# The differential branch's next V moved among the scores, and softmax scaling of three more branches moved onto the probabilities

## What is computed

```
def dense_attend(q, k, v):                       # MLA branch, 8 heads
    s = einsum('bqhd,bkhd->bhqk', q * (q.shape[-1] ** -0.5), k)
    p = softmax(s)
    return einsum('bhqk,bkhd->bqhd', p, v)

def diff_attend(q, k, v, lam):                   # differential branch, 8 heads
    s = einsum('bqhmd,bkhmd->bhmqk', q * (DIFF_HD ** -0.5), k)
    p = softmax(s)
    a = p[:, :, 0] - lam * p[:, :, 1]
    return einsum('bhqk,bkhd->bqhd', a, v)
# then rms_norm(o, subln) * (1 - lam_init)

# swa branch: 16 query heads on 4 key heads, window 128, a sink in the softmax
yz = y * silu(z);  terms += sigmoid(g) * (yz @ w_branch[r])
```

## Time and profile before

| | |
|---|---|
| time, median of 3 runs | 4425.87 us (4422.62 to 4426.99) |
| the profiled execution | 4427.5 us |
| its span in the profile | 4425.7 us |
| TensorE busy | 3882.1 us, 88% (21165 matmuls) |
| weight loads busy | 2965.3 us, 67% |
| VectorE busy | 2101.5 us, 47% (3225 instructions) |
| ScalarE busy | 1384.6 us, 31% (2472 instructions) |
| GpSimd busy | 0.2 us |
| mean granted TensorE clock | 0.946 |
| moved by DMA | 275.36 MB |

### The profile page before, as it was taken

How to read it: one execution, slowest core, us unless ns; L and a number is a source line. 1 busy time by engine, 2 the same in 40 slices (tenths; PEclk the granted TensorE clock), 3 DMA queues, 4 the chain that set the end, 5 groups by cost and what they waited for, 6 DMA issues and landing times. The chain is left out here.

```text
span 4425.7 us, 56278 instructions
## 1 busy us (share of the span) xinstructions
PE 3882.1 (88%) x21165; PEld 2965.3 (67%) x21165; DVE 2101.5 (47%) x3225; ACT 1384.6 (31%) x2472; POOL 0.2 (0%) x4
## 2 busy tenths in 40 slices
PE   5988979996699999999798998977999999798888
PEld 2665758874466787777586766765667666585666
DVE  2444345543444425667524554333453666535544
ACT  2433233322133313444312433221332444313432
POOL 0000000000000000000000000000000000000000
PEclk8999989998799999999899999988999999899999
DMA  6443325531101021111121101211103111131122
GB/s 231 132 120 86 95 85 167 166 104 53 29 24 28 24 62 39 33 38 38 29 62 34 29 25 34 62 40 35 32 27 86 42 44 43 38 76 34 34 56 73
DMA packets 504242, 275.36 MB, mean 62 GB/s; under 512 B 56666, under 2 KB 489782, under 8 KB 504095
## 3 DMA queue, kind: packets, MB, share of 16 engines
q1 hardware_dynamic: 483186, 252.08, 20.3%
q10 hardware_dynamic: 20908, 21.26, 1.5%
HBM read 271.08 MB, written 10.32 MB: 64 GB/s over the span
## 5 line engine op out<-in xcount | busy, mean ns | idle before, releaser
L559 PE MATMUL ps<-h_high,w_high 128*128 128x512 f32 (+1 forms) x3512 | 1334.6, 380 | 187.3 <-DVEq L2249 130.7
L559 PE MATMUL ps<-h_low,w_high 128*128 128x512 f32 (+1 forms) x3512 | 1282.5, 365 | 0.0
L559 PE MATMUL ps<-h_high,w_low 128*128 128x512 f32 (+1 forms) x3512 | 1279.0, 364 | 0.0
L559 PEld LDWEIGHTS ps<-h_high,w_high 128*128 128x128 f32 x3512 | 673.8, 192 | 349.4 <-DVEq L2249 137.9
L555 DVE TENSOR_TENSOR w_low<-w_raw,w_high 128x1024 fp32r<-128x1024 f32 x378 | 453.6, 1200 | 626.8 <-ACT w_high L545 606.9
L559 PEld LDWEIGHTS ps<-h_low,w_high 128*128 128x128 f32 x3512 | 674.9, 192 | 105.6 <-issue 11.7
L559 PEld LDWEIGHTS ps<-h_high,w_low 128*128 128x128 f32 x3512 | 673.2, 192 | 106.6
L545 ACT ACTIVATE w_high<-w_raw 128x1024 fp32r<-128x1024 f32 x378 | 392.4, 1039 | 796.3 <-PE ps L559 610.0
L778 ACT ACTIVATE probs<-ps,neg_max 128x768 f32<-128x768 f32 (+2 forms) x368 | 288.8, 788 | 469.5 <-DVE neg_max L803 268.7
L559 PE MATMUL ps<-k_high,q_high 64*128 64x256 f32 (+4 forms) x784 | 189.9, 403 | 152.5 <-ACT probs L778 100.9
L559 PE MATMUL ps<-probsT,v 128*128 128x512 f32 (+4 forms) x736 | 286.9, 559 | 5.2 <-DVE probsT L986 4.8
(11 more groups left out here) (197 smaller groups left out, 3948.4 us busy)
## 6 DMA issues: line engine op xcount, KB each, us to landing
w_raw<-in_w_in SPq DMA_DIRECT2D x444, 256.0 KB, 3.1
y_and_merged<-in_w_mod SPq DMA_DIRECT2D x96, 256.0 KB, 3.1
w_raw<-in_w_branch SPq DMA_DIRECT2D x96, 256.0 KB, 3.1
w_raw<-in_w_up SPq DMA_DIRECT2D x88, 256.0 KB, 4.2
y_and_merged<-in_w_ada SPq DMA_DIRECT2D x64, 256.0 KB, 3.4
w_raw<-in_w_out SPq DMA_DIRECT2D x48, 256.0 KB, 3.1
w_raw<-in_w_down SPq DMA_DIRECT2D x44, 256.0 KB, 2.9
y_and_merged<-in_w_ada SPq DMA_DIRECT2D x4, 2048.0 KB, 20.4
```

Of the source, the lines that this page charges most:

```text
L559: return nc.tensor.matmul(*a, **kw)
```

## The change

Two parts. First, `SCALED_LAST` holds `swa` alone. `dil`, `na` and `mla` so go the way of `diff`: each item's probabilities are scaled by VectorE before they are transposed, one item behind the maxima (in pairs in the twin branches), the waits before the values are for `normed`, and the spreading matmuls, the common reciprocal and the multiplication of Z are gone for them. Second, in `diff` the 16 steps of the next V stand behind Q and K in the side work of the scores: 48 steps instead of 32 in layer 0, 40 instead of 24 in layer 1. To free PSUM banks 0 and 1 for them, ScalarE copies Q out amid the exponentials, behind the item at which `side_plan` has the Q steps done (`act_q_out`, semaphore `q_out`); the rotation of Q goes to bank 3; V's features go to a slot of YM instead of EB. ScalarE copies V after the first chunk's copy; the transposes of V stand right behind the value products, then the sums of squares, then Z's projection. On VectorE the copy of V's transposes comes ahead of the output. The epilogues have no side work, before and after.

```diff
-SCALED_LAST = ("dil", "na", "mla", "swa")
+SCALED_LAST = ("swa",)
...
                 maxima(idx)
-            inverses()
+                if idx and s["name"] not in SCALED_LAST:
+                    normalise(idx - 1)
+            if s["name"] in SCALED_LAST:
+                inverses()
+            else:
+                normalise(n - 1)
...
-            pe.wait_ge(S["exped"], cnt(s, "exped", t, per * s["items"], (u + 1) * s["items"]))
+            if s["name"] in SCALED_LAST:
+                pe.wait_ge(S["exped"], cnt(s, "exped", t, per * s["items"], (u + 1) * s["items"]))
+            else:
+                pe.wait_ge(S["normed"], cnt(s, "normed", t, per * s["items"], (u + 1) * s["items"]))
...
-            spread_inverses(pe, s, t, u)
+            if s["name"] in SCALED_LAST:
+                spread_inverses(pe, s, t, u)
             product(n - 1)
-            if s["cq"]:
+            if s["name"] in SCALED_LAST and s["cq"]:
                 spread_context(pe, s)
...
-            at = min([g for g in range(s["items"] // size) if done_by(s, q + k, g) >= q] + [s["items"]])
-            return q + k, size * (at + 1)
+            v = 16 if s["name"] == "diff" else 0
+            at = min([g for g in range(s["items"] // size) if done_by(s, q + k + v, g) >= q] + [s["items"]])
+            return q + k + v, size * (at + 1)
...
+            b = 3 if name == "diff" else 0
+            mm(PS[0:rows, 512 * b:512 * b + 512], rot[:, :], Q[0:rows, 0:LAT], start=True, stop=True).then_inc(S["rope_mm"], 1)
...
+                pe.wait_ge(S["q_out"], cnt(s, "q_out", t, ui, u + 1))
                 yield from split_steps(pe, s, t, 4, 2, 128, tgroups(0, True))
...
-            return PP[:, 4096:4608] if s["first"] else EB[:, 1, :]
+            return PP[:, 4096:4608] if s["first"] else YM[:, 13 * TOK:14 * TOK]
...
+        def act_q_out(act, s, t, u):
+
+            act.wait_ge(s_h, cnt(s, "h", t, 4, 1))
+            for d, p in evac_cols(s, 0, Q, s["cq"]):
+                last = act.activation(d, p, ACT.Copy, scale=SCALE["diff"])
+            last.then_inc(S["q_out"], 1)
...
             if s["first"]:
                 yk = i + (0 if name == "dil" else 4)
-                v.tensor_tensor(Y[:, yk, 0:LAT], bank(5), Z[:, 0:LAT], ALU.mult).then_inc(S["y"], 1)
+                v.tensor_copy(Y[:, yk, 0:LAT], bank(5)).then_inc(S["y"], 1)
...
+            def qkv_steps(t, u, i):
+                yield from qk_steps(pe, nxt, t, u, i + 1, True)
+                yield from v_steps(pe, nxt, t, u, i + 1)
...
+                if name == "diff":
+                    pe_scores(pe, s, t, u, i, 0, qkv_steps(t, u, i), n_side)
+                    pe_values(pe, s, t, u, i, 0, lambda: pe_rope(pe, nxt, t, u, name))
+                    pe_turn_v(pe, nxt, t, u)
+                    pe_oss(pe, s, t, u, i)
+                    pe_proj_z(pe, nxt, t, u, i + 1)
+                    return
...
+                    if name == "diff" and idx == side_plan(s)[1] - 1:
+                        act_q_out(act, nxt, t, u)
...
+                        if c == 0 and name == "diff":
+                            act_proj_v(act, nxt, t, u, i + 1)
...
+                if name == "diff":
+                    dve_proj_v(dve, nxt, t, u, i + 1)
                 dve_output(dve, s, t, u, i, 0)
-                dve_proj_v(dve, nxt, t, u, i + 1)
+                if name != "diff":
+                    dve_proj_v(dve, nxt, t, u, i + 1)
```

More of the change, by code:

```diff
@@ L151, in add @@
             now[k] = now.get(k, 0) + v
-    keys = ("h n square square_mm rstd scaled high x_t mm_ev rope_in rope_mm roped q_mm k_mm kv_ev vt_in vt_mm v_ev z_ev tanh scores maxed exped normed "
+    keys = ("h n square square_mm rstd scaled high x_t mm_ev rope_in rope_mm roped q_mm k_mm q_out kv_ev vt_in vt_mm v_ev z_ev tanh scores maxed exped normed "
             "pt_act pt_dve rl_mm transposed o_done o_sq o_ss o_rs y bias merged up_ev gelu f_high f_low y_low y_high m_high m_low out_ev ctx_in mod_copy mod_sum qk_high qk_low").split()
@@ L178, in plan @@
             if s["name"] == "diff":
-                add(s, vt_in=n, vt_mm=n, v_ev=n, z_ev=n, tanh=n, rope_mm=2 * n, roped=2 * n, o_sq=n, o_ss=n, o_rs=n)
+                add(s, vt_in=n, vt_mm=n, v_ev=n, z_ev=n, tanh=n, rope_mm=2 * n, roped=2 * n, q_out=n, o_sq=n, o_ss=n, o_rs=n)
             if s["name"] == "swa":
@@ L942, in product @@
                     last = mm(o, v, turned(s, c, j, 128 * len(tiles))[1], start=start, stop=stop, skip_group_check=True)
-                if c == n - 1 and not s["cq"]:
+                if c == n - 1 and not (s["cq"] and s["name"] in SCALED_LAST):
                     last.then_inc(S["o_done"], 1)
-            pe.wait_ge(S["exped"], cnt(s, "exped", t, per * s["items"], (u + 1) * s["items"]))
+            if s["name"] in SCALED_LAST:
+                pe.wait_ge(S["exped"], cnt(s, "exped", t, per * s["items"], (u + 1) * s["items"]))
+            else:
+                pe.wait_ge(S["normed"], cnt(s, "normed", t, per * s["items"], (u + 1) * s["items"]))
             if s["first"]:
@@ L1058, in pe_rope @@
             pe.wait_ge(S["rope_in"], cnt(s, "rope_in", t, ui, u + 1))
-            mm(PS[0:rows, 0:512], rot[:, :], Q[0:rows, 0:LAT], start=True, stop=True).then_inc(S["rope_mm"], 1)
+            b = 3 if name == "diff" else 0
+            mm(PS[0:rows, 512 * b:512 * b + 512], rot[:, :], Q[0:rows, 0:LAT], start=True, stop=True).then_inc(S["rope_mm"], 1)
             if nr == 2:
@@ L1072, in v_steps @@
                 return
-            pe.wait_ge(S["roped"], cnt(s, "roped", t, ui * (2 if name == "diff" else 1), (u + 1) * (2 if name == "diff" else 1)))
             if name == "mla":
+                pe.wait_ge(S["roped"], cnt(s, "roped", t, ui, u + 1))
                 k = plain_slot(s, t, 2, u)
@@ L1126, in act_proj_qk @@
                 act_high(act, s, t, per, 1)
-            act.wait_ge(s_h, cnt(s, "h", t, per, 1))
-            for d, p in evac_cols(s, 0, QH if s["first"] else Q, cq):
-                last = act.activation(d, p, ACT.Copy, scale=sc)
+            if name != "diff":
+                act.wait_ge(s_h, cnt(s, "h", t, per, 1))
+                for d, p in evac_cols(s, 0, QH if s["first"] else Q, cq):
+                    last = act.activation(d, p, ACT.Copy, scale=sc)
+            elif first:
+                act_q_out(act, s, t, u)
             if name == "swa":
@@ L1208, in dve_proj_qk @@
             if name == "diff":
-                dve_rope(dve, s, 2 * u, t, 2 * ui, Q[:, 0:LAT], 128, 0, TAB["cos_hd"][:, :], TAB["sin_hd"][:, :])
+                dve_rope(dve, s, 2 * u, t, 2 * ui, Q[:, 0:LAT], 128, 3, TAB["cos_hd"][:, :], TAB["sin_hd"][:, :])
                 dve_rope(dve, s, 2 * u + 1, t, 2 * ui, KB[:, 0, 0:LAT], 128, 2, TAB["cos_hd"][:, :], TAB["sin_hd"][:, :])
@@ L1350, in moved @@
             m.base = dict(s.base)
-            for key, per in (("h", s["nh"]), ("n", s["nn"]), ("v_ev", 1), ("vt_in", 1), ("vt_mm", 1), ("z_ev", 1), ("rope_in", 1), ("tanh", 1), ("kv_ev", 1),
+            for key, per in (("h", s["nh"]), ("n", s["nn"]), ("v_ev", 1), ("vt_in", 1), ("vt_mm", 1), ("z_ev", 1), ("q_out", 1), ("rope_in", 1), ("tanh", 1), ("kv_ev", 1),
                              ("qk_high", 1), ("qk_low", 1), ("roped", 2 if s["name"] == "diff" else 1), ("rope_mm", 2 if s["name"] == "diff" else 1), ("y", s["subs"])):
@@ L1518, in step, with mid @@
             def step(t, u, i):
-                act_exps(act, s, t, u, i, 0, splits(s, nxt, t, u, 0), (lambda idx: swa_z(t, u, i, idx)) if name == "swa" else lambda idx: None)
+                def mid(idx):
+                    if name == "swa":
+                        swa_z(t, u, i, idx)
+                    if name == "diff" and idx == side_plan(s)[1] - 1:
+                        act_q_out(act, nxt, t, u)
+                act_exps(act, s, t, u, i, 0, splits(s, nxt, t, u, 0), mid)
                 if s["first"]:
@@ L1538, in step @@
                     act_osq(act, s, t, u, i)
-                act_proj_v(act, nxt, t, u, i + 1)
+                else:
+                    act_proj_v(act, nxt, t, u, i + 1)
                 if s["first"]:
```

3 lines of the change are left out of this document (1 added, 2 removed).

## The result

| | kernel before | changed kernel |
|---|---|---|
| time, median | 4426.26 us (4 runs) | 4351.89 us (4348.03 to 4354.65, 4 runs) |
| ratio | | 0.9833, 95% interval 0.9821 to 0.9844 |
| profiled execution | 4427.5 us | 4348.03 us |
| its span | 4425.7 us | 4346.2 us |
| TensorE busy | 3882.1 us | 3848.7 us (20877 matmuls) |

The change takes 74.4 us, the forecast was 67. TensorE lost only 33 us of busy time: most of the gain is idle time.

What follows compares the result with a forecast made beforehand. TensorE was taken as the bound, with holes, in the differential units. From 4427.5 us, less 4.3, 16.5, 15.75 and 30.1, came 4360.9, or 4359 against the median; range 4335 to 4392.

Steps and rivals of the forecast that it cites:

- Part 1, steady units: First block and MLA: steady units gain the whole spreading, 0.92 us, 1.33 (MLA layer 0) and 0.89 (MLA layer 1).
- MLA's two last units expose about 1.1 us ... 0.5 us better each: Last MLA unit of each layer: exposed scaling against removed spreading and Z multiplication, a gain of 1.0 us in all.
- 0.6 us worse each: First block's two last units: bare scalings add about 1.5 us for 0.92 removed, 1.2 us lost in all.
- Part 2, steady units: Differential branch: V's steps fill TensorE's holes, gaining 2.25 us a unit in layer 0 and 4.3 in layer 1.
- the last chunk's copy: Layer 0 differential value phase: copy queued behind q_low and k_low leaves a 0.55 us wait, chosen between 0 and 1.9.
- the switch of matmul kinds: Differential units, both layers: one more switch between kinds of matmul costs 0.15 us a unit.
- the estimate of 1.7 less 0.4: Layer 1 differential units: slow stretch after idling costs 1.7 us, less 0.4 because the mean unit is shorter.
- Last units of the branch have no next V and keep their time: End of each differential stage: the last unit's time does not change.
- (a): Differential value phase gives the gain back as VectorE's queue becomes the bound there: 4388 us, chance 0.12.
- (b): TensorE's clock falls in the bare differential value phase, making it slower: 4443 us at 6 us a unit, chance 0.04.
- (c): The change does not act because a semaphore holds V back until the exponentials end: 4405 or 4424 us, chance 0.08.
- (d): All holes in the differential units close: 4336 us, chance 0.04.

Runs made afterwards that it cites:

- part 2 alone: Kernel before with only the V steps moved among the scores of the differential branch: 4363.39 us, ratio 0.9857.
- both edits: Changed kernel, first MLA unit's V projection not awaiting rotation, inverse sums spread as before in last dil, na and layer 1 MLA units: 4341.58 and 4340.46 us.

## Why the prediction was right, point by point

The direction, the mechanism of each part and the range held (4335 to 4392, measured 4351.9). The sum was 7 us short because two errors of opposite sign stood in it, some 8 us too much for part 1 and 18 too little for part 2, so that it came this close is in part luck.

- **Part 1, steady units: right.** MLA lost 1.33 and 0.96 us a unit (forecast 1.33 and 0.89), the first block 0.7 to 1.0 (0.92). TensorE waits for no scaling there. The pair of reciprocal and scaling at 512 columns, taken from the slope as 0.63 us, is 0.63 in the timeline of VectorE:

```profile
354.30 0.49 DVE L821 TENSOR_SCALAR probs<-probs,exp_sum_inv 128x512 f32<-128x512 f32 x1
...
354.93 0.49 DVE L821 TENSOR_SCALAR probs<-probs,exp_sum_inv 128x512 f32<-128x512 f32 x1
```

- **Part 1, last units: mis-sized.** The step "MLA's two last units expose about 1.1 us ... 0.5 us better each" held in layer 0 (0.7 better) and failed in layer 1: 2.0 us worse. I counted only the scaling behind the last exponential; the scalings between the maxima also delay the last maximum and so the last exponential (it starts 3.98 us behind the start of the last pair's scores instead of 3.39), and the clock fell behind the longer wait. "0.6 us worse each" in the first block was about 1 in `na`, 0.7 to 0.9 in four traces of `dil`, and up to 2 us more in the stretch behind `dil`, which no term held: the forecast of 4.3 us for the first block came to nothing that the traces or the time show. Part 1 measured 12.5 us alone, forecast 20.8.
- **The rule against part 1.** The advice of the Trainium skill to minimise VectorE instructions ("VectorE: DVE Perf Modes", Rules for kernel authors) was weighed as a price for each instruction. The pair costs just what the row said; what it cost beyond hung on whether TensorE had other work.
- **Part 2, steady units: right, layer 0 a little too careful.** 2.76 us against 2.25: the last chunk's copy left 0.2 and not 0.55; the switch of matmul kinds shows no wait, and no run measures its 0.15 by itself. Layer 1: 4.24 against 4.3; the clock's share was 1.0, where the estimate of 1.7 less 0.4 made it 1.3. The unit that was read held 1.2 us of clock (50.96 less 49.72) and not 1.7, and the others from nothing to 1.4.
- **Part 2, ahead of the first unit: a missing term.** "Last units of the branch have no next V and keep their time" spoke of the stage's end, and nothing of its start, though the diff replaces V's wait for `roped` by one for `q_out` there as well. It is worth 5 us in each layer, which the kernel with that wait put back shows. With it, 0.6 x 7 more in layer 0 and last units that were 1.1 and 0.4 us shorter in the trace of part 2 alone (not forecast, and not tested) some 61 of the 63.6 us come together that part 2 measured; forecast 45.85.
- **The rivals.** (a) did not come: waits in the value phase and behind it are 1.3 us in layer 0 and 1.1 in layer 1, under the 2.5 that would have decided. (b) did not come: the clock is 1.00 in both units, transposes and products included. (c) did not come. (d) would have needed those waits to be nothing.

## What to carry to other kernels

A wait that an edit replaces must be looked up at every place that shares the code: the pass ahead of the loop has the same instructions and no side work to hide them, and 5 us a stage were lying there. A cover of side work ends with the last unit: cost that unit by itself, with every instruction that delays the last exponential. Idle time of TensorE cost more than its length here in most units, so filling it even with useless matmuls paid, and moving real work into it paid more. And one unit is a poor sample where the clock moves: compare the same row in several units, and in several traces, before a price is taken from it.

## What the runs showed of the hardware

A wait of 2.8 us in each unit of layer 1 cost another 1.0 us on the mean through the granted clock, which useless matmuls in that hole gave back. What a wait costs beyond its length changes with the same instructions and the same wait. Within one trace it cost nothing to 1.4 us a unit. Between two traces of the changed kernel the matmuls behind 3.54 us of waiting started at the full clock in one (0.39 us) and at the low clock in the other (0.63). The Trainium skill ("TensorE: Matmul & The Clock Gate", What's actually happening) says that the number of slow matmuls varies from run to run with the phase of the gate; the rows of these two traces agree. That such places make up all of the 6 us by which runs of one kernel differ (4348.0 to 4354.7) is likely, not shown.

Between kernels the difference can be a lasting one. Behind 2.08 us of waiting in the last MLA unit of layer 1 the unit took 24.6 us in all three traces without part 1 in MLA, 26.1 with the old way put back into it, and 28.0 in both traces with both edits. So an edit in one stage moved the price of an idle stretch in another; by what it did so isn't shown.
